# A hybrid attention and gated DeltaNet block on one Trainium2 core: raw queries and keys with reciprocal norms as factors, and a new order of the tiles' work

## What is computed

```python
dq = l2_normalize(dq.reshape(B, S, DN_HEADS, DN_HEAD_DIM))     # 4 heads of 128
dk = l2_normalize(dk.reshape(B, S, DN_HEADS, DN_HEAD_DIM))
...
# per chunk of 64 tokens; decay from the cumulated g; q is scaled by Dk ** -0.5
m_low = where(strict, einsum('bhncd,bhned->bhnce', k * beta, k) * decay, 0.0)
t_inv = triangular_solve(eye + m_low, eye)
u = t_inv @ (v * beta)
w = t_inv @ (k * beta * exp(g))
a_intra = einsum('bhncd,bhned->bhnce', q, k) * decay
# scan over the chunks
v_new = u_c - w_c @ state
o = (q_c * exp(g_c)) @ state + a_c @ v_new
state = state * exp(g_last) + (k_c * exp(g_last - g_c)).T @ v_new
...
o_dn = o_dn * rsqrt(mean(o_dn * o_dn, axis=-1) + RMS_EPS) * dn_norm_w * silu(dz)
```

## Time and profile before

| what | us |
|---|---|
| median of 3 runs | 1577.75 (1576.59 to 1582.75) |
| the profiled execution | 1581.23 |
| its span, first to last instruction | 1579.4 |
| PE busy (matmuls) in the span | 1499.2 |
| VectorE busy | 840.6 |
| ScalarE busy | 446.5 |
| GpSimd busy | 329.1 |

### The profile page before, as it was taken

How to read it: one execution, slowest core, us unless ns; L and a number is a source line. 1 busy time by engine, 2 the same in 40 slices (tenths; PEclk the granted TensorE clock), 3 DMA queues, 4 the chain that set the end, 5 groups by cost and what they waited for, 6 DMA issues and landing times.

```text
span 1579.4 us, 22891 instructions
## 1 busy us (share of the span) xinstructions
PE 1499.2 (95%) x8790; PEld 1224.8 (78%) x8790; DVE 840.6 (53%) x1550; ACT 446.5 (28%) x1024; POOL 329.1 (21%) x345
## 2 busy tenths in 40 slices
PE   8999999897897898899999899999999999999996
PEld 7888887676676676677888778888888888888885
DVE  3565224555555555545444853334333377777778
ACT  3222132322322322224311221122211244444540
POOL 3666434222222212213391200000000000000000
PEclk9999999999999899999999999999999999999998
DMA  7222432331231231212462324444443276565422
GB/s 202 79 94 106 146 117 72 91 88 60 70 88 55 75 88 47 65 56 100 158 215 92 120 100 160 139 148 163 151 160 134 79 260 216 158 191 169 138 76 107
DMA packets 103992, 190.84 MB, mean 121 GB/s; under 512 B 10640, under 2 KB 50640, under 8 KB 101584
## 3 DMA queue, kind: packets, MB, share of 16 engines
q1 hardware_dynamic: 94960, 170.01, 33.4%
...
## 4 chain that ended last, share of the span: by engine, by line
PE 85%; DVE 10%; issue 2%; ACT 1%; DMA 0%; ACTq 0%; DVEq 0%; SPq 0%
PE ps L1527 14%; PE ps L1528 14%; PE ps L1529 14%; PE ps L1592 12%; PE ps L1923 6%; PE ps L1922 6%; PE ps L1921 6%; PE ps L1661 3%; PE ps L1600 3%; PE ps L1538 1%; PE ps L1739 1%; PE ps L1731 1%; PE ps L1693 1%; PE ps L1742 1%; PE ps L1720 1%
## 5 line engine op out<-in xcount | busy, mean ns | idle before, releaser
L1527 PE MATMUL ps<-x,slh 128*128 128x512 f32 x512 | 200.2, 391 | 2.3 <-DVE x L1359 1.8
L1529 PE MATMUL ps<-x,sll 128*128 128x512 f32 x512 | 200.0, 391 | 0.0
L1528 PE MATMUL ps<-x,slh 128*128 128x512 f32 x512 | 199.8, 390 | 0.0
L655 POOL TENSOR_TENSOR ring2l<-raw,ring2h 128x256 fp32r<-128x256 f32 x180 | 176.2, 1008 | 3.6
L1923 PE MATMUL ps<-thi,slow 128*128 128x512 f32 x416 | 161.9, 389 | 0.0
L1921 PE MATMUL ps<-thi,shi 128*128 128x512 f32 x416 | 161.8, 389 | 0.0
L1922 PE MATMUL ps<-tlow,shi 128*128 128x512 f32 x416 | 161.8, 389 | 0.0
L1398 DVE TENSOR_TENSOR hq<-hq 128x512 f32<-128x512 f32 x64 | 44.3, 692 | 209.9 <-ACT hq L982 209.9
L1592 PE MATMUL ps<-xh,ring2l 128*128 128x512 f32 x304 | 128.0, 421 | 0.0
L652 POOL CAST ring2h<-raw 128x1024 fp32r<-128x1024 f32 x45 | 48.2, 1070 | 379.8 <-PE ps L1592 233.5
L1592 PE MATMUL ps<-xh,ring2h 128*128 128x512 f32 x304 | 126.0, 414 | 0.0
...
## 6 DMA issues: line engine op xcount, KB each, us to landing
...
sraw<-hpark SPq DMA_DIRECT2D x104, 256.0 KB, 2.8
...
```

What stands on the lines that cost most here:

```text
L655: ins = pool.tensor_tensor(lo[:, k:k + 2, :], src[:, k:k + 2, :], hi[:, k:k + 2, :].bitcast(F32), ALU.subtract)
L1527: mm(outp, lh, rh, start=start, stop=False)
L1528: mm(outp, lh, rl, start=False, stop=False)
L1529: return mm(outp, ll, rh, start=False, stop=stop)
```

## The change

Queries and keys are no longer normalised. `dqk` holds q and k as loaded (channels on the partitions, two buffers), and `a_kk` and `a_kq` read them at once; `a_trn`, the ScalarE copies of its result and VectorE's `qn` and `kn` are gone. The reciprocal norms are factors for each token: `brs` (beta times the norm of k, and times its square) goes into `vb`, `eml` and the recurrence's factor, `rqs` (the norm of q) into `b_on`. For that the squares of q are taken from a copy with the chunks exchanged, `dqs`, and k is loaded once more into `kq`. `b_ds` is parted into `b_ds` and `b_o`, `a_r` into `a_tb` and `a_r`, `a_d` into `a_d` and `a_em`. The order of all three `step` functions is new, and `full` too. Of the `step` functions the diff shows the lines that are there after; the removed ones stand in the code above.

SyncE, the loads:

```diff
+            def load_a(t, p):
                 if isinstance(t, int) and t == 0:
                     for q in range(2):
                         sp.wait_ge(dn_out[q], 8 * N_DN)
                 else:
...
+                    sp.wait_ge(vb_ok, t)
+                sp.dma_start(dqk[p][:, :, :], park[0:2 * NH, :, bass.ds(PAD + t * P, P)].rearrange("b p s -> p b s")).then_inc(dn_in, 16)
+                for c in range(2):
+                    sp.dma_start(dqs[:, :, (1 - c) * CH:(2 - c) * CH],
+                                 park[0:NH, :, bass.ds(PAD + t * P + c * CH, CH)].rearrange("b p s -> p b s")).then_inc(dn_in, 16)
...
+            def load_ks(t, p):
+                if not (isinstance(t, int) and t == 0):
+                    sp.wait_ge(ks_mm, 2 * t - 1)
+                for c in range(2):
+                    sp.dma_start(kq[p][:, :, 3 * c, :], park[NH:2 * NH, :, bass.ds(PAD + t * P + c * CH, CH)].rearrange("b p s -> p b s")).then_inc(ks_in, 16)
```

ScalarE:

```diff
-            def a_kt_qt(t, p):
-                act.wait_ge(tkn_mm, t + 1)
-                cp(kq[p][:, :, 0:4:3, :], A1[:, :].rearrange("p (h c i) -> p h c i", h=NH, c=2))
-                act.wait_ge(tqn_mm, t + 1)
-                cp(qt[:, :, :], A0h).then_inc(qt_ok, 1)
...
                 if t is not None: b_vn(t, 0)
+                if a is not None: a_t1(a, p)
+                fill(0)
                 if t is not None: b_exps(t, 0)
+                if t is not None: b_vn(t, 1)
                 if t is not None: b_pt(t, 0)
...
                 if t is not None: b_ya(t, 0)
...
+                if n is not None: a_scalars(n, 1 - p)
                 if t is not None: b_osq(t)
                 if t is not None: b_exps(t, 1)
...
                 if n is not None: a_eg(n)
...
+                if n is not None: a_squares_q(n)
+                if t is not None: b_pt(t, 1)
                 fill(1)
...
+                fill(2)
                 if n is not None: a_squares_k(n)
                 if t is not None: b_ya(t, 1)
...
                 fill(3)
+                if n is not None: a_exps(n)
```

VectorE:

```diff
+            def a_norm(t, p):
+                dve.wait_ge(sqq_ok, t + 1)
+                dve.wait_ge(sqk_ok, t + 1)
+                chain(dve.tensor_scalar(ssa[:, :], ssa[:, :], RMS_EPS, None, ALU.add))
+                newton(ssa[:, :], nwy[:, :], nwt[:, :])
+                tt(brs[:, 0:NH], sc(p, G_BETA), nwy[:, NH:2 * NH], ALU.mult)
+                chain(dve.tensor_scalar(rqs[p][:, 0:NH], nwy[:, 0:NH], QSCALE, None, ALU.mult))
+                tt(rqs[p][:, NH:2 * NH], rqs[p][:, 0:NH], rqs[p][:, 0:NH], ALU.mult)
+                chain(tt(brs[:, NH:2 * NH], brs[:, 0:NH], nwy[:, NH:2 * NH], ALU.mult))
+                chain(dve.scalar_tensor_tensor(out=sc(p, G_NBEG), in0=brs[:, NH:2 * NH], scalar=-1.0, in1=sc(p, G_EG), op0=ALU.mult, op1=ALU.mult))
+            def a_ee(t):
                 dve.wait_ge(e_ok, t + 1)
-                tt(eml[:, :, :], eml[:, :, :], bc(sc(p, G_BETA), CH), ALU.mult).then_inc(ee_ok, 1)
+                tt(eml[:, :, :], eml[:, :, :], bc(brs[:, NH:2 * NH], CH), ALU.mult).then_inc(ee_ok, 1)
                 dve.wait_ge(ee_ok, 2 * t + 1)
                 tt(em0[:, :, :], eml[:, :, :], bh(msk(M_L0)), ALU.mult).then_inc(ee_ok, 1)
-            def a_norm(t):
-
-                dve.wait_ge(sq_ok, t + 1)
-                chain(dve.tensor_scalar(ssa[:, :], ssa[:, :], RMS_EPS, None, ALU.add))
-                newton(ssa[:, :], nwy[:, :], nwt[:, :])
-                chain(dve.tensor_scalar(nwy[:, 0:NH], nwy[:, 0:NH], QSCALE, None, ALU.mult))
-
-            def a_qn(t):
-                tt(qn[:, :, :], C0h, bc(nwy[:, 0:NH], P), ALU.mult).then_inc(qn_ok, 1)
-
-            def a_kn(t, p):
-                chain(tt(kn[:, :, :], C1h, bc(nwy[:, NH:2 * NH], P), ALU.mult))
-                tt(kdec[p][:, :, :], kn[:, :, :], bc(sc(p, G_EGL), P), ALU.mult).then_inc(kn_ok, 1)
+            def a_kd(t, p):
+                dve.wait_ge(sqk_ok, t + 1)
+                tt(kdec[p][:, :, :], C1h, bc(sc(p, G_EGL), P), ALU.mult).then_inc(kd_ok, 1)
             def a_vb(t, p):
                 dve.wait_ge(trv_mm, t + 1)
-                tt(vb[p][:, :, :], C0h, bc(sc(p, G_BETA), P), ALU.mult).then_inc(vb_ok, 1)
-
-            def a_eargs(t, p):
-
-                dve.wait_ge(qt_ok, t + 1)
+                tt(vb[p][:, :, :], C0h, bc(brs[:, 0:NH], P), ALU.mult).then_inc(vb_ok, 1)
+            def a_qeg(t, p):
                 dve.wait_ge(eg_ok, t + 1)
-                tt(kq[p][:, :, 1:3, :].rearrange("p h a c -> p h (a c)"), qt[:, :, :], qeg[:, :, :], ALU.mult).then_inc(qegt_ok, 1)
+                dve.wait_ge(dn_in, 48 * t + 48)
+                tt(kq[p][:, :, 1:3, :].rearrange("p h a c -> p h (a c)"), dqk[p][:, 0:NH, :], qeg[:, :, :], ALU.mult).then_inc(qegt_ok, 1)
...
-            def b_on(t):
+            def b_on(t, p):
                 dve.wait_ge(osq_ok, t + 1)
-                chain(dve.tensor_scalar(ssb[:, :], ssb[:, :], 1.0 / P, RMS_EPS, ALU.mult, ALU.add))
+                chain(dve.scalar_tensor_tensor(out=ssb[:, :], in0=ssb[:, :], scalar=1.0 / P, in1=rqs[p][:, NH:2 * NH], op0=ALU.mult, op1=ALU.mult))
+                chain(dve.tensor_scalar(ssb[:, :], ssb[:, :], RMS_EPS, None, ALU.add))
                 newton(ssb[:, :], nwu[:, :], nwv[:, :])
+                chain(tt(nwu[:, :], nwu[:, :], rqs[p][:, 0:NH], ALU.mult))
...
+                if a is not None: a_m(a, p)
+                if a is not None: a_qeg(a, p)
                 if t is not None: b_x(t, 0, 1 - p)
                 if t is not None: b_max(t, 0, 1 - p)
...
                 if t is not None: b_state(t, 0, 1 - p)
+                if a is not None: a_ys(a, 1)
+                if a is not None: a_att(a, p)
                 if t is not None: b_prob(t, 0)
                 if t is not None: b_x(t, 1, 1 - p)
...
+                if a is not None: a_tb(a, 1)
+                if a is not None: a_r(a, 1, p)
+                if a is not None: a_ys(a, 2)
                 if t is not None: b_state(t, 1, 1 - p)
...
+                if a is not None: a_tb(a, 2)
                 if a is not None: a_r(a, 2, p)
                 if a is not None: a_ys(a, 3)
...
+                if t is not None: b_max(t, 1, 1 - p)
+                if t is not None: b_on(t, 1 - p)
+                if t is not None: b_prob(t, 1)
+                if a is not None: a_tb(a, 3)
                 if a is not None: a_r(a, 3, p)
...
+                if n is not None: a_d(n, 1 - p)
                 if a is not None: a_ys(a, 4)
+                if a is not None: a_tb(a, 4)
+                if a is not None: a_r(a, 4, p)
+                if a is not None: a_ys(a, 5)
+                if n is not None: a_norm(n, 1 - p)
+                if n is not None: a_em(n)
                 if t is not None: b_yd(t)
...
                 if n is not None: a_vb(n, 1 - p)
                 if a is not None: a_r(a, 5, p)
+                if n is not None: a_ee(n)
+                if n is not None: a_kd(n, 1 - p)
```

PE:

```diff
             def a_trv(t):
-                pe.wait_ge(qn_ok, t + 1)
-                trans(C0h, lambda h: dnt[:, 2 * NH + h, :]).then_inc(trv_mm, 1)
-
-            def a_trn(t):
+                pe.wait_ge(dv_in, 16 * t + 16)
+                pe.wait_ge(sqq_ok, t + 1)
+                trans(C0h, lambda h: dv[:, h, :]).then_inc(trv_mm, 1)
+            def a_free(t):
                 if isinstance(t, int) and t == 0:
                     pe.wait_ge(uni_out, 2 * 18)
                 else:
                     pe.wait_ge(a_done, t)
-                pe.wait_ge(kn_ok, t + 1)
-                trans(A1h, lambda h: kn[:, h, :]).then_inc(tkn_mm, 1)
-                pe.wait_ge(qn_ok, t + 1)
-                trans(A0h, lambda h: qn[:, h, :]).then_inc(tqn_mm, 1)
             def a_kk(t, p):
-                pe.wait_ge(qt_ok, t + 1)
+                a_free(t)
                 for h in range(NH):
-                    for c, r in enumerate(chunks):
-                        last = mm(half(A0, 0)[r, h, :], kq[p][:, h, 3 * c, :], kq[p][:, h, 3 * c, :], start=True, stop=True)
+                    for r in chunks:
+                        last = mm(half(A0, 0)[r, h, :], dqk[p][:, NH + h, r], dqk[p][:, NH + h, r], start=True, stop=True)
                 last.then_inc(kk_mm, 1)
             def a_kq(t, p):
-                pe.wait_ge(qt_ok, t + 1)
+                a_free(t)
                 for h in range(NH):
-                    for c, r in enumerate(chunks):
-                        last = mm(half(A1, 0)[r, h, :], kq[p][:, h, 3 * c, :], qt[:, h, r], start=True, stop=True)
+                    for r in chunks:
+                        last = mm(half(A1, 0)[r, h, :], dqk[p][:, NH + h, r], dqk[p][:, h, r], start=True, stop=True)
                 last.then_inc(kq_mm, 1)
...
+            def b_o(t, c, p):
+                r = slice(c * CH, (c + 1) * CH)
+                other = slice((1 - c) * CH, (2 - c) * CH)
+                pe.wait_ge(vn_ok, 2 * t + (c + 1))
+                pe.sem_inc(waited, 1)
...
```

(93 more changed lines are left out.)

95 lines of the change are left out of this document (28 added, 67 removed).

## The result

The changed kernel takes 1541.96 us (median; 1541.57 to 1543.44), the kernel before beside it 1580.19: a ratio of 0.9761, 95% interval 0.9736 to 0.9787. That is 38 us less, where 26 were forecast. The profiled execution has a span of 1541.3 us.

The account below looks back on a forecast made before the run. TensorE was taken as the bound, its largest wait 43.8 us for VectorE's `ys`. Terms of −0.9, −1.6 and −1.1 a tile, −25 in seven, and −1 for the opening made −26: 1552 us, range 1543 to 1562, wider 1520 to 1572.

Parts of the forecast that it names:

- the loop's gap: TensorE's idle 2.3 us at the loop's turn, claimed to stay, so no gain was counted.
- rival 2: Two small VectorE operations pass per GpSimd turn: wait 2.5 us, time 1526 us; chance 0.13.
- transposes and breaks: On TensorE, eight transposes fewer (0.9 us) and nine breaks of gate runs fewer (1.6 us) a tile.
- clock behind it: TensorE's granted clock still falls to half behind the wait in nearly all tiles; no gain counted.
- opening, last tile: Opening loses transposes and eight breaks but has waits, −1 us; last tile keeps its wait at `b_pt(1)`, 0.
- The bound and the place of the new wait: TensorE's stall moves from `a_u(2)` to `a_y(4)`, 5.2 us instead of 6.3, seven times, with clock 0.50 behind it.
- Why `ys` was late: On VectorE it stands behind maximum, `a_d`, probabilities and `b_on`, whose small operations get through once per GpSimd operation.
- R: Start of VectorE's maximum, the zero from which the prediction counted the new chain's times.
- The size of the new wait: TensorE wants `a_y(4)` at R + 8.5 us, VectorE's `rinv` ends at R + 13.7: wait 5.2 us.
- the count of turns: `b_on`'s 12 small operations alternate with GpSimd's, two or three passing in its 0.4 us gap; through at R + 10.2.
- rival 3: Each small VectorE operation also holds GpSimd up for its own length: wait 7.0 us, time 1565 us; chance 0.15.
- Head and end of the tile: VectorE's work there fits inside TensorE's 7.5 us with 0.8 to spare; wait at `b_vn(0)` taken as 0.

Follow-up runs that it names:

- the late rope: Changed kernel, but GpSimd's rope of the next tile waits until VectorE has written the second half's probabilities: 1503.02 us, 0.9512 of the kernel before.
- the six added operations: Changed kernel with six more small VectorE products in `b_on`, behind its Newton step, results unused: 1565.07 us.
- the finer rope: Changed kernel with rope's two large products and four sums on GpSimd each cut in two halves, same work in all: 1532.83 us.
- the two runs: Changed kernel with the late rope: in one, three more gate runs a step, 1514.28 us; in the other, one gate run less, 1504.69 us.

## Why the prediction was right, and where it was off

The sum came out 12 us too small, and not by one error: the wait, the clock and the loop's gap gave 19 us more than forecast, the shorter work and the two end tiles 7 less. The wait of 3.5 us lies below the forecast's 4.3 to 6.0, and 1541.96 just below its 1543; the wider range of 1520 to 1572 held the time because it also took in rival 2.

The seven tiles from the first `b_ks` of tile 0 to that of tile 7 took 408.3 us before (271.9 to 680.2), 367.4 after (272.5 to 639.9), and 329.4 with the late rope (272.9 to 602.3), which has no slow clock there and no wait but one gap of 0.3. After has 24.6 of wait; over the 12 us behind each of the seven waits the granted clock is 0.76 to 0.87 in the mean, which loses 14.5, and leaves 328.3 of work, close to the late rope's 329.4. Before had 43.5 of wait and 4.8 of the loop's gap; over the 12 us behind each wait the clock is 0.74 to 0.86, which loses 17.8, and leaves 342.2 of work. That is 2.5 a tile where the prediction took 2.1: it read the slow stretch only to 489.0. With these losses the six tiles of the loop come out alike before, at 49.1 to 49.2 us of work each.

| term | predicted, us | measured, us |
|---|---|---|
| transposes and breaks | -17.5 | -13.9 (342.2 to 328.3) |
| wait | -7.7 | -18.9 (43.5 to 24.6) |
| clock behind it | 0 | -3.3 (17.8 to 14.5) |
| loop's gap | 0 | -4.8 |
| opening, last tile | -1 | +2.8 |
| sum | -26 | -38.1 |

*The bound and the place of the new wait.* Right: the stall moved from `a_u(2)` to `a_y(4)`, seven times, with the clock at 0.50 behind it. The late rope, the six added operations and the finer rope show its cause: the first two with the size expected of turns, the third with a little less (9 us, where 10 to 14 were expected).

*Why `ys` was late.* Only half right. The earlier trace rows showed slowed operations, and I took them for the whole wait. With the rope late 3.1 of the 6.3 us stay: they were VectorE's order. The change had removed this half by its new order, and the sum for after was not touched by the error, since it counts the new chain from R.

*The size of the new wait.* The mis-sized term: 5.2 predicted, 3.5 measured (with PE ready at R + 8.7, 8.5 predicted). The step that failed is the count of turns: I let small operations pass in the one gap that GpSimd's rows print in brackets, and had nine sit out a turn. GpSimd's order has two more pauses, where rope waits for its own products; seven sat out, the last of them the cast, and none met the four subtractions. Rival 2 (two a turn, wait 2.5) was too good, rival 3 (strict turns, 7.0) too bad. GpSimd is not held up by small operations: with the six added, 20 of them fell on it, 3.2 us by their own 0.16, and it took 11.52 us from rope's start to the split's end; with the late rope, when three were held, 11.54. The 11.95 of after, and the 0.80 for each of the split's four that rival 3 took as its sign, come with `pr`: the four behind rope take 3.21 where `pr` falls on them (before, after) and 2.77 to 2.81 where it does not (six added, late rope). Rival 3 was what the lock of the Trainium skill's "SBUF — State Buffer", section "SBUF: two separate sides", would do. That a blocked operation waits for a whole instruction of the other engine agrees with 0.38 beside the short sums and 0.66 beside the long ones; that the other side is blocked as long does not agree with 11.52.

*Transposes and breaks.* Too large in sum: 2.5 a tile predicted, 2.0 measured in the mean of seven, 1.7 in the six of the loop. The prices hold: a transpose 0.10 (0.109 taken), a break 0.16 to 0.17 by the two runs (0.18 taken, 1.6 / 9), together 2.2 to 2.3 a tile. What takes the rest back in the new order stays open.

*The loop's gap.* Wrong: counted as staying, it went, hidden by the 24 products ahead of the turn. Before there were 8, and I read no run length off the order there.

*Head and end of the tile.* Right: no wait at `b_vn(0)`. The last tile lost 2.2 us instead of 0: the wait for `ub` of 1.2 behind that for `pr` (2.7 together, 1.9 before), and a clock that stays at half for some 7 us, to 677, where before had some 3. In the opening 0.6 was lost, where 1 was to be gained.
